# An mLSTM projection without its RMS norm, whose scale comes in behind the product, and column sums that stream 64 columns

## The reference, cut to what matters

```python
def rmsnorm(x, g):
    y = x * rsqrt(mean(x * x, axis=-1) + EPS)
    return y * g

h = h + 0.5 * rmsnorm(swiglu(rmsnorm(h, gn[0]), w_in, w_out), gn[1])   # stage f0
u = rmsnorm(h, gn[2])                                                  # the norm in question
z  = u @ w_in                                                          # 3088 columns
qk = silu(causal_conv(z[..., :1024], conv_w, conv_b))                  # 4 taps over the tokens
v  = z[..., 1024:2048]
og = z[..., 2048:3072]
gates = z[..., 3072:] + gate_b                                         # 8 input, 8 forget gates
y  = mlstm(q, k, v, input gates, log_sigmoid(forget gates)) * sigmoid(og)
h = h + rmsnorm(y @ w_out, gn[3])                                      # stage a
h = h + 0.5 * rmsnorm(swiglu(rmsnorm(h, gn[4]), w_in, w_out), gn[5])   # stage f1
```

## Time and profile before

| | |
|---|---|
| median of 3 runs | 806.78 us (806.22 to 808.01) |
| the profiled execution | 806.2 us, its span 804.2 us |
| mean granted TensorE clock of it | 0.992 of full speed |
| busy, share of the span | PE 99%, weight loads 96%, DVE 74%, ACT 52%, POOL 18% |
| DMA queues | 157.85 MB in 45120 packets, 59.1% of 16 engines' span |

### The profile page before, as it was taken

How to read it: one execution, slowest core, us unless ns; L and a number is a source line. 1 busy time by engine, 2 the same in 40 slices (tenths; PEclk the granted TensorE clock), 3 DMA queues, 4 the chain that set the end, 5 groups by cost and what they waited for, 6 DMA issues and landing times.

```text
span 804.2 us, 15615 instructions
## 1 busy us (share of the span) xinstructions
PE 795.3 (99%) x6338; PEld 771.1 (96%) x6338; DVE 594.5 (74%) x952; ACT 416.5 (52%) x710; POOL 143.6 (18%) x159
## 2 busy tenths in 40 slices
PE   9999999999999999999999999999999999999997
PEld 9999999999999999999999999999899999999986
DVE  6877777698786976778777779996667568567753
ACT  7444444454367565565444445536555454555541
POOL 3800000041320000020000004230245302035510
PEclk9999999999899999999999999999999999999999
DMA  9876777695436632559867679546544651744531
GB/s 342 308 250 226 233 247 249 204 325 178 122 112 215 192 130 81 182 175 298 287 218 266 241 239 339 177 145 211 163 151 129 185 161 53 264 154 133 157 106 52
DMA packets 45190, 158.83 MB, mean 197 GB/s; under 512 B 5040, under 2 KB 6576, under 8 KB 45120
## 3 DMA queue, kind: packets, MB, share of 16 engines
q1 hardware_dynamic: 45120, 157.85, 59.1%
HBM read 156.76 MB, written 1.06 MB: 196 GB/s over the span
## 4 chain that ended last, share of the span: by engine, by line
PE 97%; issue 1%; DVE 1%; POOL 0%; ACT 0%; DVEq 0%; POOLq 0%
PE ps L313 26%; PE ps L315 25%; PE ps L314 25%; PE ps L665 3%; PE ps L354 2%; PE ps L358 2%; PE ps L355 2%; PE ps L366 2%; PE ps L329 1%; PE ps L557 1%; PE ps L629 1%; PE ps L648 1%; PE ps L638 1%; PE ps L691 1%; PE ps L689 1%
## 5 line engine op out<-in xcount | busy, mean ns | idle before, releaser
L1032 DVE TENSOR_TENSOR w<-raw,w 128x1024 fp32r<-128x1024 f32 x245 | 300.0, 1238 | 132.6 <-ACT w L738 132.2
L313 PE MATMUL ps<-u,w 128*128 128x256 f32 (+1 forms) x1231 | 353.2, 287 | 0.0
L315 PE MATMUL ps<-u,w 128*128 128x256 f32 (+1 forms) x1231 | 349.6, 284 | 0.0
L314 PE MATMUL ps<-u,w 128*128 128x256 f32 (+1 forms) x1231 | 349.0, 284 | 0.0
L738 ACT CAST w<-raw 128x1024 fp32r<-128x1024 f32 x245 | 254.0, 1049 | 122.4 <-PE ps L315 102.7
L313 PEld LDWEIGHTS ps<-u,w 128*128 128x128 f32 x1231 | 232.0, 188 | 6.2 <-issue 4.3
L315 PEld LDWEIGHTS ps<-u,w 128*128 128x128 f32 x1231 | 232.3, 189 | 0.0
L314 PEld LDWEIGHTS ps<-u,w 128*128 128x128 f32 x1231 | 231.7, 188 | 0.0
L313 PE MATMUL ps<-h,w 128*128 128x272 f32 (+1 forms) x352 | 99.7, 283 | 0.0
L314 PE MATMUL ps<-h,w 128*128 128x272 f32 (+1 forms) x352 | 99.3, 282 | 0.0
L315 PE MATMUL ps<-h,w 128*128 128x272 f32 (+1 forms) x352 | 99.1, 282 | 0.0
(11 more groups left out here) (246 smaller groups left out, 1043.1 us busy)
## 6 DMA issues: line engine op xcount, KB each, us to landing
raw<-wst SPq DMA_DIRECT2D x245, 512.0 KB, 4.6
adr<-wada SPq DMA_DIRECT2D x48, 512.0 KB, 4.0
Bt<-bias_rows SPq DMA_DIRECT2D x8, 192.0 KB, 3.9
hT<-xT SPq DMA_DIRECT2D x4, 272.0 KB, 4.5
outT<-yg SPq DMA_DIRECT2D x4, 256.0 KB, 2.0
cs<-cst SPq DMA_DIRECT2D x1, 140.0 KB, 5.3
cs<-cst SPq DMA_DIRECT2D x1, 128.0 KB, 6.5
vc<-vec SPq DMA_DIRECT2D x1, 101.0 KB, 3.7
```

Source lines behind the costliest of these rows:

```text
L313: e.matmul(out, a, x1, start=first, stop=False)
L314: e.matmul(out, a, x2, start=False, stop=False)
L315: return e.matmul(out, b, x1, start=False, stop=last)
L1032: e.tensor_tensor(w2[:, k % NW, :], raw[:, k % NRAW, :], w1[:, k % NW, :].bitcast(F32), ALU.subtract).then_inc(*tick(s_split, k))
```

## The change

It does four things. (1) Between f0 and a, `weighed` takes the place of `normalised`: u is h times gain, r2 is worked out and spread while the head runs. (2) The factor r2 is brought in behind the projection: VectorE multiplies qk j and the gate rows with it as it takes them from PSUM (in place of ScalarE's copy to `zp` and VectorE's copy of the gates); for v, the factor is transposed once to one number per partition (`rv`), and ScalarE multiplies it on as it takes the transposed v from PSUM (in place of VectorE's copies L1320, L1321); for og, ScalarE copies the block out, GpSimd multiplies by r0, and ScalarE takes tanh after that. (3) TensorE no longer waits for r2 ahead of the mixer. (4) `column_sums` streams each column of `wts` 64 times over, so a matmul of it has 64 or 128 moving columns where it had 1 or 2; readers of the sums take every 64th.

```diff
@@ tensor
-            def column_sums(b, src, n, w, cols, first, last):
-                tt = sum_tiles(n)
-                for j, (a, z) in enumerate(tt):
-                    m = e.matmul(ps[0:z - a, b, cols[j]:cols[j] + w[1] - w[0]], src[:, a:z], wts[:, w[0]:w[1]],
-                                 start=first and j == 0, stop=last, skip_group_check=True)
+            def column_sums(b, src, n, w, col, first, last):
+
+                for j, (a, z) in enumerate(sum_tiles(n)):
+                    many = wts[:, w[0]:w[1]].unsqueeze(2).broadcast_to([P, w[1] - w[0], 64])
+                    o = 128 * j + col
+                    m = e.matmul(ps[0:z - a, b, o:o + 64 * (w[1] - w[0])], src[:, a:z], many, start=first and j == 0,
+                                 stop=last, skip_group_check=True)
...
+                dense(4)
+                e.wait_ge(s_pow.handle, at(s_pow, ("r1", "f0")))
+                spread(("r1", "f0"), 6, T, rst)
+
+                def spread_scale(i):
+                    if i == KT // 2:
+                        e.wait_ge(s_pow.handle, at(s_pow, ("r2", "f0")))
+                        spread(("r2", "f0"), 5, T, rst2)
+
+                def scale_columns():
+
+                    b = place(("rv",), 6)
+                    e.wait_ge(*read(("r2", "f0")))
+                    for j, (a, z) in enumerate(tok_tiles(T)):
+                        m = e.transpose(ps[0:z - a, b, 128 * j:128 * j + 128], r0[:, a:z], ident)
+                    m.then_inc(*tick(s_rvtr, 0))
...
-                head(keys[:3], c, x1, x2, T, *u_of("a"))
+                head(keys[:3], c, x1, x2, T, *u_of("a"), hook=spread_scale)
                 for j in range(8):
                     if j:
                         block(("qk", j), c + 1 + 2 * j, x1, x2, T)
+                        if j == 1:
+                            scale_columns()
                         block(("v", j), c + 2 + 2 * j, x1, x2, T)
                         v_transpose(j - 1)
...
-            both_scales("f0", T)
             mlstm()
@@ scalar
             def mlstm():
                 c = C_A
-                e.wait_ge(s_zero.handle, 1)
+
+                def v_scaled(h):
+
+                    b = bank_of(("vt", h))
+                    e.wait_ge(s_vtr.handle, at(s_vtr, h))
+                    if h == 0:
+                        e.wait_ge(s_pad.handle, at(s_pad, "last"))
+                        e.wait_ge(*read(("rv",)))
+                    for j, n in enumerate((P, P, NMETA)):
+                        m = e.mul(Vs[0:n, j, h, 0:128], ps[0:n, b, 128 * j:128 * j + 128], rv[0:n, j:j + 1])
+                    m.then_inc(*reading(("vt", h)))
+
                 split_to(c + NW - 1)
                 for j in range(8):
                     i = j % 2
                     if j:
                         split_to(c + 1 + 2 * j + NW - 1)
-                    proj(("qk", j))
-                    if j > 1:
-                        e.wait_ge(s_cv.handle, at(s_cv, (j - 2, 2)))
-                    e.copy(zp[:, i, 3:3 + T], out_of(("qk", j), T)).then_inc(*tick(s_zp, j))
-                    e.mul(cv[:, i, :], out_of(("qk", j), T), a_tap(3, j)).then_inc(*reading(("qk", j)))
+                    e.wait_ge(*read(("qk", j)))
+                    e.mul(cv[:, i, :], zp[:, i, 3:3 + T], a_tap(3, j)).then_inc(*tick(s_cvm, j))
                     if j:
                         split_to(c + 2 + 2 * j + NW - 1)
                     proj(("v", j))
                     if j > 1:
                         e.wait_ge(s_vtr.handle, at(s_vtr, j - 2))
                     e.copy(vT[:, i, :], out_of(("v", j), T)).then_inc(*reading(("v", j)))
+                    if j:
+                        v_scaled(j - 1)
...
-                    e.activation(og[:, h, :], out_of(("og", h)), ACT.Tanh, scale=0.5).then_inc(*reading(("og", h)))
+                    e.copy(og[:, h, :], out_of(("og", h))).then_inc(*reading(("og", h)))
+
+                def gate_tanh(h):
+                    e.wait_ge(s_ogs.handle, at(s_ogs, h))
+                    e.activation(og[:, h, :], og[:, h, :], ACT.Tanh, scale=0.5).then_inc(*tick(s_tanh, ("og", h)))
...
                 gate_block(1)
+                v_scaled(7)
                 for h in range(NH):
                     if h < NH - 2:
                         gate_block(h + 2)
                     if 0 < h < NH - 2:
                         output(h - 1)
                     sums_over_keys(h)
+                    gate_tanh(h)
                     if h % 2 == 0 and h < NH - 2:
                         weights(h // 2 + 1)
...
-            normalised("f0", T, None)
+            weighed("f0", "a", T, 2)
@@ vector
             def mlstm():
                 c = C_A
-                e.wait_ge(s_spread.handle, at(s_spread, ("r2", "f0")))
                 e.memset(zp[:, :, 0:3], 0.0).then_inc(*tick(s_zero, 0))
-                split_to(c + NW - 1)
                 proj(("gates",))
+                e.wait_ge(*read(("r2", "f0")))
                 b = bank_of(("gates",))
-                e.tensor_scalar(gi, ps[0:8, b, 0:T], vc[0:8, V_GB:V_GB + 1], None, ALU.add).then_inc(*tick(s_gate, "i"))
-                e.tensor_copy(fx_, ps[32:40, b, 0:T]).then_inc(*reading(("gates",)))
+                e.tensor_tensor(gi, ps[0:8, b, 0:T], r0[0:8, :], ALU.mult).then_inc(*tick(s_gate, "zi"))
+                e.tensor_tensor(fx_, ps[32:40, b, 0:T], r0[32:40, :], ALU.mult).then_inc(*reading(("gates",)))
+                e.wait_ge(s_gate.handle, at(s_gate, "zi"))
+                e.tensor_scalar(gi, gi, vc[0:8, V_GB:V_GB + 1], None, ALU.add).then_inc(*tick(s_gate, "i"))
...
-                def v_copied(h):
...
                 for j in range(8):
                     i = j % 2
                     if j:
                         split_to(c + 1 + 2 * j + NW - 1)
-                    e.wait_ge(s_zp.handle, at(s_zp, j))
+                    proj(("qk", j))
+                    if j > 1:
+                        e.wait_ge(s_cv.handle, at(s_cv, (j - 2, 2)))
+                    e.tensor_tensor(zp[:, i, 3:3 + T], out_of(("qk", j), T), r0, ALU.mult).then_inc(*reading(("qk", j)))
+                    if j == 1:
+                        e.wait_ge(s_rvtr.handle, 1)
+                        e.tensor_copy(rv[:, 0:2], ps[:, 6, 0:256:128])
+                        e.tensor_copy(rv[0:16, 2:3], ps[0:16, 6, 256:257]).then_inc(*reading(("rv",)))
                     for tap in range(3):
                         if tap == 0:
-                            e.wait_ge(*read(("qk", j)))
+                            if j == 0:
+                                e.wait_ge(s_zero.handle, 1)
+                            e.wait_ge(s_cvm.handle, at(s_cvm, j))
...
                     if j:
                         split_to(c + 2 + 2 * j + NW - 1)
-                        v_copied(j - 1)
...
                 def output(h):
+                    e.wait_ge(s_tanh.handle, at(s_tanh, ("og", h)))
                     e.wait_ge(s_ytr.handle, at(s_ytr, h))
...
-                v_copied(7)
...
-            normalised("f0", "a", T, lambda k: norm_gain(2, k), None, eps0)
+            weighed("f0", "a", T, 2, C_A, eps0)
@@ gpsimd
-            boundary("f0", T)
-            e.wait_ge(s_spread.handle, at(s_spread, ("r2", "f0")))
+            first_power("f0", T)
+            h_added("f0", T, (2,))
+            second_power("f0", T)
+            h_added("f0", T, (3, 5, 6, 7))
+            e.wait_ge(s_spread.handle, at(s_spread, ("r1", "f0")))
...
+            for h in range(NH):
+                e.wait_ge(*read(("og", h)))
+                if h == 0:
+                    e.wait_ge(*read(("r2", "f0")))
+                e.tensor_tensor(og[:, h, :], og[:, h, :], r0[:, 16:T], ALU.mult).then_inc(*tick(s_ogs, h))
```

More of the change, by code:

```diff
@@ L125, in build @@
         rst2 = sb("rst2", [P, 4])
+        rv = sb("rv", [P, 4])
         tmp = sb("tmp", [P, 4, T])
@@ L489, in mixer_out @@
                 place(("sumc", s), 5)
-                column_sums(5, sqa[:, 2, :], S, W_TWO, SUM_C, True, False).then_inc(*tick(s_colsum, ("early", s)))
+                column_sums(5, sqa[:, 2, :], S, W_TWO, SUM_Y, True, False).then_inc(*tick(s_colsum, ("early", s)))
                 row_sums(7)
                 e.wait_ge(s_hy.handle, at(s_hy, (s, "hy", 7)))
-                column_sums(5, hyg[:, 1, :], S, W_TWO, SUM_C, False, True).then_inc(*tick(s_colsum, ("sumc", s)))
+                column_sums(5, hyg[:, 1, :], S, W_TWO, SUM_Y, False, True).then_inc(*tick(s_colsum, ("sumc", s)))
             def both_scales(s, n, rows_of_gains=False):
@@ L1006, in scalar @@
             ffn_out(0, "f0", T)
[L1007 removed]
+            weighed("f0", "a", T, 2)
             mlstm()
[L1009 removed]
+            weighed("a", "f1", S, 4)
             split_to(C_F[1] + NW - 1)
@@ L1116, in first_input @@
                 e.wait_ge(s_colsum.handle, at(s_colsum, ("sum", "x")))
-                e.tensor_scalar(sst[:, 0:2], ps[:, 7, 0:4:2], EPS, None, ALU.add)
```

(37 more changed lines are left out.)

37 lines of the change are left out of this document (14 added, 23 removed).

## The result

The changed kernel takes **819.13 us** (median of 4 runs, 818.92 to 819.3) against 806.59 for the kernel before on the same chip (806.22 to 808.01, 4 runs): a ratio of 1.0155, 95% interval 1.0142 to 1.0168. It is 12.5 us slower. The forecast was 814.5, 7.7 slower, with 818.0 as the upper end.

What follows compares the result with a forecast made beforehand. TensorE's stream, 97% of the chain, was taken as the bound. Span 804.2 + 8.6 lateness (including -1.4) - 0.9 = 811.9, 813.9 profiled, 814.5 us median; own range 811.5 to 817.5, stated range 808.0 to 818.0.

Steps and rivals of the forecast that it cites:

- Handover f0 to a: From the first stage's head to the layers: last u2 written at 225.65 instead of 227.04, -1.4 us.
- 64 or 128 columns cost nothing: Column sums: wider passes cost nothing beside the weight load; taken as 0, bounds 0 and 0.02 us a pass (1.9).
- Handover a to f1: Before the second FFN: wide sums hold the clock at 1.00 and the spread comes sooner, -0.9 us, bounds 0 and -1.7.
- The mixer's loop: Rounds 1 to 7 become serial chains on ScalarE and VectorE, +7.6 us; start -0.3, so ScalarE is late by 7.3.
- The 0.78 of scalings: Mixer rounds: three new ScalarE scalings of v at 0.26 us each, counted in the round's serial chain.
- What reaches TensorE: Mixer: waits at chunk 71, v 4 to 6, first sums and heads make TensorE 8.6 us late at the output projection.
- For the heads: Mixer heads: lateness grows from 5.8 to 7.5 us at head 1's numerators, plus 1.1 over three later pairs.
- GpSimd's products at nothing: Mixer gates: GpSimd's eight products, some 0.7 us each, are hidden and their collisions with VectorE cost 0, bound 3.2 us.
- Faster: Rival: the mixer's rounds stay hidden, TensorE waits for nothing and only the handovers count, 804.5 us; chance 0.12.
- half: Rival: ScalarE catches up or v's scalings are cheaper, late by 2 to 5 us, 808 to 811; chance 0.15.
- The clock never fell in a wait of the mixer: Rival: the clock falls in the new waits, up to 1.7 us one or two times, 815 to 818; chance 0.15.
- the wide sums don't hold the clock: Rival: the a to f1 handover gains nothing, 815.4 us, inside the forecast's range; no separate chance given.

Runs made afterwards that it cites:

- fifth kernel: The changed kernel with the tile rv moved behind the mixer's last tile, so later tiles keep the addresses of the kernel before: 816.08 us.
- the second: The changed kernel with column sums of one moving column instead of 64: 818.92 us, ratio 1.0156 to the kernel before.
- the sixth: The kernel before with an unused tile of 16 bytes a partition (taking 32) where the change puts rv: 809.2 us, ratio 1.0039.
- the seventh: The kernel before with u1 and u2 rows of 1280 bytes and all moving tiles begun 64 bytes above a multiple of 256: 793.67 us, ratio 0.9846.
- The ninth: The kernel before with 64 unused bytes ahead of its first tile, so all tiles, weights included, lie 64 bytes higher: 806.13 us, ratio 0.9996.
- third kernel: The changed kernel with VectorE's multiply of qk by r0 ahead of its subtraction in each mixer round: 811.7 us, ratio 1.0067 to the kernel before.
- eleventh kernel: The fifth kernel with v's scaling done by two VectorE instructions instead of three of ScalarE: 816.23 us against 816.08.
- twelfth kernel: The third kernel without the gate blocks' scale (no ScalarE copy, no GpSimd products), so its result differs: 810.26 us against 811.7.
- the first: The kernel before with the column sums of 64 moving columns and nothing else of the change: 806.6 us, ratio 1.0004.
- the fourth: The changed kernel with sums of 16 moving columns instead of 64: 818.14 us, ratio 1.0146 to the kernel before.
- the eighth: The changed kernel with the edits of third kernel, the fourth and fifth kernel, plus chunk 71's cast and subtraction and each tanh moved earlier: 806.38 us.

## Why the prediction was wrong

The direction, the main mechanism and the places of the waits were right; the size was off by 4.8 us (7.7 forecast, 12.5 measured). The step that failed is the premise that a matmul of TensorE costs what it cost before, so that only waits and handovers need a price. The fifth kernel divides the miss: 816.1, 9.8 above the kernel before and inside the range, is the change without its shifted addresses.

- **Outside the sum: +2.7 to 3.0 us.** The prediction says that TensorE's stream is the time and prices what makes TensorE wait. It took the price of a matmul as fixed. The 32 bytes of `rv` changed that price in h, m and y, which the change doesn't name. The matmuls of h in the second FFN took 118.3 ns instead of 113.6. No term and no bound stood for it, and the upper end of 818.0 was passed by 1.1.
- **Handover f0 to a, costed at -1.4: failed.** In the fifth kernel the last u2 was written at 226.58, 0.5 earlier than before instead of 1.4. The chain from first `scaled` to last u2 came out as estimated (216.25 to 227.65 is 11.40 in the changed kernel, estimate 11.4). Its start was late: the sums took 0.6 more, the four fillers 0.58 instead of 0.4, and the first stage was 0.2 late before that; in all the last u2 came 0.9 later than forecast. So "64 or 128 columns cost nothing" was the wrong end of its bounds. A pass costs 0.12 to 0.13 with 64 columns and 0.16 with 128, from 0.11; the upper bound of 0.02 a pass was a little low (0.6 for 24 passes). The forecast had taken the price from transposes with 128 columns, 0.11 each, and a sum with 128 columns didn't keep it; why the two differ was not tested.
- **Handover a to f1, costed at -0.9:** -0.7 (the offset goes from 10.3 to 9.6 in the fifth kernel), and the clock there is 1.00. But the reason given doesn't stand as the only one, so the hit is in part luck. Three kernels with the old narrow sums had 1.00 there too (the second, the sixth and the seventh), and the sixth, which is the kernel before and 32 unused bytes, gained the same 0.7. The ninth, with 64 unused bytes, had 0.56.
- **The mixer's loop, +7.6 less 0.3: right.** From the last u2 to the cast behind round 7 the forecast had 59.2 us; measured 59.5. Round by round, 1 to 7, it had +1.3, +0.4, +2.3, +1.3, +0.6, +0.5 and +1.2; the casts of the changed kernel give +1.3, +0.4, +2.3, +1.2, +0.5, +0.5 and +1.2. Only the way to round 1 was longer, 6.85 instead of 6.3. The third kernel shows the cause: moving one instruction takes 7.4 of the 12.5 us away. The 0.78 of scalings is a smaller part than the sum made it (eleventh kernel): the chain has a second branch, VectorE's, of nearly the same length.
- **What reaches TensorE: right.** Ahead of chunk 71 and of the transposes of v 4 to 6 waits of 0.7, 2.25, 1.0 and 1.2 were forecast; the starts there lay 1.25, 2.19, 1.04 and 1.29 us apart in the fifth kernel, each with a slot of some 0.12 in it. The first sums over keys began at 291.99 in the changed kernel, 8.0 later than in the earlier trace rows; less the 2.0 by which its loop started behind the forecast that is 6.0, forecast 5.8. For the heads I had 1.7 and 1.1; the trace has three waits, 2.4 together. From the first sums to the mixer's end the fifth kernel lost 3.3 us, forecast 2.8.
- **GpSimd's products at nothing: right for the time.** They took 1504 ns each instead of the 0.7 that I read from four others, and the twelfth kernel prices copy, product and wait at 1.4 us, which the two waits on ScalarE's late numerators explain. The forecast had GpSimd wait for a weight subtraction, and it did; the 0.2 us in each of four subtractions for y stayed hidden. The Trainium skill, "SBUF — State Buffer", section "SBUF: two separate sides", has the later of the two engines block fully. The rows fit that with GpSimd as the later one: each product ends 0.6 us behind the subtraction into which it started.
- **Rivals.** Faster and half fell at the wait ahead of v 4. The clock never fell in a wait of the mixer, 1.9 us the longest. It was 1.00 at both handovers, so "the wide sums don't hold the clock" fell too.

## What to carry to other kernels

When a scale is moved behind a product, count the handoffs, not the work: the same instructions cost 7.4 us more when one of them stands behind its engine's subtraction than ahead of it. Where TensorE is the bound, compare how many matmuls it starts in equal windows of untouched stages before reading any wait; a new tile of a few bytes can move every later one, so put it behind the others. And try the starts and row lengths of moving tiles as a parameter of their own: here they were worth 12.6 us, as much as the change cost.

## What the hardware showed

- **The slot of a matmul (from its start to the start of the next) depends on where its operands lie.** For 256 columns of fp32r it was 113.6 ns or 118.3, with clock, load and waits equal, and it changed with 32 bytes (113.6 to 118.3 for h, 117.8 to 119.9 for m). Rows of 1280 bytes with a start at 64 modulo 256 gave u 113.4 in the second FFN, but both 113.3 and 117.7 in the layers, and 119.7 where it is read 64 bytes further on (117.4 before). With rows of 1088 bytes the remainder runs through four values from row to row, and so do the distances: 115 to 122 ns, repeating every 12 matmuls, in the second FFN's input phase. The same remainder doesn't do the same for 272 columns (123.3 at best), and moving all tiles together changes nothing. Which distance counts (to the weights, to the other moving tile, to the rows before) was not separated, nor was the start from the row length for u. The Trainium skill, "TensorE: Matmul & The Clock Gate", section "Wait — 56ns, not 53.3ns?", has matmuls back to back at N / 2.4 GHz + about 2.5 ns; an estimate from that is 109 for 256 columns. The rows here, each with its weight load, lie 4 to 11 ns above it and vary by address.
- **A pass of few columns costs by its columns early.** With its own weight load: 0.11 us for 1 or 2 columns, 0.11 to 0.12 for 16, 0.12 for 32, 0.12 to 0.13 for 64, 0.16 for 128.
- **Wide sums hold the clock at f0 to a; at a to f1 other things do too.** The changed kernel and the first, third, fifth, eleventh and twelfth, all with sums of 64 columns, had 1.00 at both handovers, and the mean clock of every one of their executions was 0.997 or more. Executions of the usual length with sums of one or two columns had 0.989 to 0.996. With 16 columns the fourth had 0.78 at f0 to a and the eighth 1.00. With sums of one or two columns the clock over 214.6 to 221.5 was 0.54 in the ninth kernel and 0.75 in the second:

```profile
214.60:221.50 6.90, 6.40 (x29) 5.83 (x28) 6.08 (x15) 1.68 (x4) 3.02 (x4) 0.54 0.00 0
341.00:344.50 3.50, 3.31 (x17) 2.88 (x16) 2.76 (x9) 1.02 (x2) 0.44 (x2) 0.56 0.50 144
```

These two rows are the ninth kernel's. The sixth, the same list with 32 bytes instead of 64, has in the second place

```profile
341.50:345.00 3.50, 2.72 (x21) 2.38 (x21) 2.82 (x9) 1.02 (x2) 0.50 (x2) 1.00 0.55 142
```

So at a to f1 the kernel stands on an edge. But each profile is one execution, and the 15 executions of the kernel before on one chip had mean clocks from 0.991 to 0.996: whether the bytes or the execution decided between these two is not shown. All of it was worth 0.6 to 0.7 us at a to f1, and nothing that could be seen at f0 to a, where VectorE and ScalarE pace the head.
